# Where the sample states are read: one pass behind the projection, or two halves inside it

## What is computed

```python
S_new = jnp.exp(b_last)[..., None] * S + jnp.einsum('bshk,bshv->bhkv', k_dec, vc)
o_inter = jnp.einsum('bthk,bhkv->bthv', qc * jnp.exp(b), S)
```

## Time and profile before

| | |
|---|---|
| median of 3 runs | 1629.11 us (1628.82 to 1630.61) |
| profiled execution | 1628.45 us |
| its span | 1626.7 us |
| TensorE busy | 1551.4 us, 95% |
| VectorE, ScalarE, GpSimd busy | 1280.9, 976.4, 148.4 us |
| mean DMA rate | 274 GB/s |
| mixer of layer 0, projection and output | about 17 to 170 us |
| mixer of layer 1 | about 392 to 545 us |
| experts | from about 586 us on |

### The profile page before, as it was taken

One profiled execution on the slowest core, in us unless ns is written; L12 is line 12 of the kernel. 1 busy time (PEld: TensorE's weight loads), 2 busy tenths in 40 slices (PEclk: granted clock), 3 DMA queues, 4 the chain that ended last, 5 costly groups with the idle time before them and its releaser, 6 DMA issues.

```text
span 1626.7 us, 23700 instructions
## 1 busy us (share of the span) xinstructions
PE 1551.4 (95%) x8504; PEld 1330.3 (82%) x8504; DVE 1280.9 (79%) x1192; ACT 976.4 (60%) x832; POOL 148.4 (9%) x115
## 2 busy tenths in 40 slices
PE   7989899998999969999999999999999999999996
PEld 6989899998989858778788788787787787887884
DVE  6874666656575368989989989989989888888885
ACT  6463433334454256776776776676776676677672
POOL 2000560000000000200200200200200200200100
PEclk9997999999997879999999999999999999999999
DMA  9451676454433159999999999999999999999990
GB/s 305 141 169 37 215 229 203 155 179 132 155 107 109 53 204 339 366 359 344 366 361 336 359 364 340 364 368 338 355 370 346 349 366 341 349 366 351 344 388 29
DMA packets 216397, 445.21 MB, mean 274 GB/s; under 512 B 7568, under 2 KB 63304, under 8 KB 216352
## 3 DMA queue, kind: packets, MB, share of 16 engines
q1 hardware_dynamic: 208480, 421.72, 72.9%
q0 software_dynamic: 4960, 16.47, 3.2%
q10 hardware_dynamic: 2912, 6.42, 1.3%
HBM read 437.58 MB, written 7.06 MB: 273 GB/s over the span
## 4 chain that ended last, share of the span: by engine, by line
PE 73%; DVE 11%; issue 9%; ACT 4%; DMA 2%; ACTq 0%; DVEq 0%; POOLq 0%; SPq 0%
PE ps L1474 22%; PE ps L1476 21%; PE ps L1475 21%; DVE w_lo L873 7%; ACT w_hi L532 2%; PE ps L1646 2%; DMA raw<-in_moe_w_dram 1%; PE ps L1550 1%; PE ps L1839 1%; PE ps L1499 1%; DVE ex_g L1386 1%; DVE xT L1375 1%; ACT ex_silu L807 1%; PE ps L1799 0%; PE ps L1751 0%
## 5 line engine op out<-in xcount | busy, mean ns | idle before, releaser
L873 DVE TENSOR_TENSOR w_lo<-raw,w_hi 128x2048 fp32r<-128x2048 f32 x401 | 941.5, 2364 | 174.5 <-ACT w_hi L532 172.2
L532 ACT ACTIVATE w_hi<-raw 128x2048 fp32r<-128x2048 f32 x401 | 762.6, 1917 | 257.2 <-PE ps L1476 210.8
L1474 PE MATMUL ps<-w_hi,xg 128*128 128x512 f32 x896 | 360.6, 402 | 11.3 <-DVE w_lo L873 10.0
L1475 PE MATMUL ps<-w_lo,xg 128*128 128x512 f32 x896 | 352.4, 393 | 0.0
L1476 PE MATMUL ps<-w_hi,xg 128*128 128x512 f32 x896 | 352.3, 393 | 0.0
L1474 PE MATMUL ps<-h_hi,w_hi 128*128 128x264 f32 x736 | 216.1, 294 | 18.4 <-DVE h_lo L921 8.4
L1474 PEld LDWEIGHTS ps<-w_hi,xg 128*128 128x128 f32 x896 | 169.1, 189 | 55.9 <-DVE w_lo L873 22.2
L1476 PE MATMUL ps<-h_hi,w_lo 128*128 128x264 f32 x736 | 211.0, 287 | 0.0
L1475 PE MATMUL ps<-h_lo,w_hi 128*128 128x264 f32 x736 | 211.0, 287 | 0.0
L1476 PEld LDWEIGHTS ps<-w_hi,xg 128*128 128x128 f32 x896 | 168.8, 188 | 37.8
L1475 PEld LDWEIGHTS ps<-w_lo,xg 128*128 128x128 f32 x896 | 169.4, 189 | 33.0
(11 more groups left out here) (299 smaller groups left out, 1604.9 us busy)
## 6 DMA issues: line engine op xcount, KB each, us to landing
raw<-in_moe_w_dram SPq DMA_DIRECT2D x336, 1024.0 KB, 6.0
raw<-in_ffn_w_dram SPq DMA_DIRECT2D x33, 1024.0 KB, 5.4
raw<-in_w_in_dram SPq DMA_DIRECT2D x24, 1024.0 KB, 5.9
raw<-in_w_out_dram SPq DMA_DIRECT2D x8, 1024.0 KB, 5.0
vb<-v_rows_scratch POOLq DMA_DIRECT2D x16, 256.0 KB, 5.1
out_dram<-hstate POOLq DMA_DIRECT2D x2, 2048.0 KB, 12.7
hstate<-in_state_hgrn_dram POOLq DMA_DIRECT2D x1, 2048.0 KB, 11.3
x_rows<-in_x_prompt_dram SPq DMA_DIRECT2D x1, 1024.0 KB
```

Of the source, the lines that this page charges most:

```text
L532: act.activation(w_hi[:, s, :], raw[:, r, :], ACT.Copy).then_inc(hi_made, 1)
L873: dve.tensor_tensor(w_lo[:, s, :], raw[:, r, :], w_hi[:, s, :].bitcast(F32), ALU.subtract).then_inc(split, 1)
L1474: pe.matmul(out, l_hi, r_hi, start=start, stop=False)
L1475: pe.matmul(out, l_hi, r_lo, start=False, stop=False)
```

## The change

Level k still stands behind unit 6 + k up to level 5. The reads become two halves of four samples. The first stands behind level 4 of unit 10, the second behind level 5 of unit 11, and each has a turn among banks 0 to 3; ScalarE evicts the results to a small tile (`states_out`). A half is 1 MB and lies in `half_state`, where the token-major values and keys will stand later, so GpSimd can load it early: the first half ahead of the mixer (in layer 1 after the final state of layer 0 is done), the second when the first is read. ScalarE's load is gone. The reload for the new states of layer 1 is issued by GpSimd behind the first gather of the experts. Levels 6 and 7 stand ahead of the transposes of the values; VectorE's low parts of units 13 and 14 move behind a gate product and behind the prompt's gate products; the gate product with the root (L1153) moves ahead of the last widening; the sums of squares stand ahead of the final state. Two waits fall away: TensorE's for the samples' outputs ahead of the merges and ScalarE's for the reads ahead of the next norm. The diff, with its context cut:

```diff
--- before.py
+++ after.py
@@ -60,7 +60,7 @@
-GATES_BEHIND = {7: (0, 1), 8: (2, 3, 4), 9: (5, 6, 7)}
+GATES_BEHIND = {7: (0, 1), 8: (2, 3, 4), 9: (5, 6, 7), 10: ("states",), 11: ("states too",)}
 TILE_TURN, GATE_TURN = [], {}
@@ -68,6 +68,7 @@
 TURNS = len(TILE_TURN) + len(GATE_TURN)
+STATE_TURN = [GATE_TURN["states"], TURNS - 1]
@@ -144,6 +145,7 @@
         vrow = at("vrow", end("xc"), [HEADS * P])
+        half_state = at("half_state", end("sc"), [NSAMPLE // 2 * HEADS, P])
         s_fin = at("s_fin", end("xc"), [HEADS, P])
@@ -203,6 +205,7 @@
         tmp = small[:, 48:160]
+        o_s = tmp[:, 0:32].rearrange("p (h b) -> p h b", h=HEADS)
         key_s = small[:, 168:200].rearrange("p (h b) -> p h b", h=HEADS)
@@ -420,6 +423,14 @@
             def mixer(l):
+                if l:
+                    pool.wait_ge(fin_done, l)
+                for half in range(2):
+                    if half:
+                        pool.wait_ge(st_read, NSAMPLE * l + NSAMPLE // 2)
+                    pool.dma_start(half_state[:, :, :],
+                                   state_hgrn[l, 4 * half:4 * half + 4].rearrange(
+                                       "b h k v -> k (b h) v")).then_inc(st_landed, 16)
                 pool.wait_ge(vrow_ready, l + 1)
@@ -488,8 +499,10 @@
             pool.wait_ge(y_done, 2 * DC + DC * FF_STEPS)
-            pool.wait_ge(st_read, NSAMPLE * DEPTH)
+            pool.dma_start(hstate[:, :, :], state_hgrn[1].rearrange("b h k v -> k (b h) v")
+                           ).then_inc(st_again, 16)
             values_begin(1)
+            pool.wait_ge(st_again, 32)
             pool.wait_ge(blocks_ready, 1)
@@ -579,8 +592,6 @@
             def norm_hi(n):
-                if n == 1:
-                    act.wait_ge(st_read, NSAMPLE)
                 for c in range(DC):
@@ -615,6 +626,18 @@
+                def states_out(half):
+                    bank = ps[:, STATE_TURN[half] % 4, :]
+                    act.wait_ge(z_done, TURNS * l + STATE_TURN[half] + 1)
+                    ins = act.activation(o_s[:, :, 4 * half:4 * half + 4],
+                                         bank[:, 0:16].rearrange("p (h b) -> p h b", h=HEADS),
+                                         ACT.Copy)
+                    if half == 0:
+                        ins.then_inc(act_step, 1)
+                        steps[0] += 1
+                        ins = act.activation(tmp[:, 64:96], bank[:, 32:64], ACT.Copy)
+                    ins.then_inc(z_free, 1)
+
                 if l:
@@ -624,7 +647,12 @@
                     for n in GATES_BEHIND.get(u - SPLIT, ()):
-                        gate(n)
+                        if n == "states":
+                            states_out(0)
+                        elif n == "states too":
+                            states_out(1)
+                        else:
+                            gate(n)
                     if l == 0 and u == SPLIT - 1:
@@ -668,12 +696,6 @@
                         act.activation(zx[:, :, :], zx[:, :, :], ACT.Sqrt).then_inc(om_root, 1)
-                    if u == IN_UNITS + SPLIT - 1:
-
-                        act.wait_ge(used, ib + IN_UNITS)
-                        act.dma_start(hstate[:, :, :],
-                                      state_hgrn[l].rearrange("b h k v -> k (b h) v")
-                                      ).then_inc(st_landed, 16)
                 act.wait_ge(v_turned, l + 1)
@@ -1098,7 +1120,7 @@
                 for u in range(IN_UNITS + SPLIT):
-                    if u >= EARLY[l]:
+                    if EARLY[l] <= u <= IN_UNITS:
                         lo(ib + u)
@@ -1145,12 +1167,13 @@
                                                ALU.mult))
-
+                        lo(ib + u)
+
+                dve.wait_ge(om_root, l + 1)
+                link(dve.tensor_tensor(lev[0][:, :, :], lev[0][:, :, :], zx[:, :, :], ALU.mult))
                 widen(7, queries_too=False)
-                dve.wait_ge(om_root, l + 1)
-                link(dve.tensor_tensor(lev[0][:, :, :], lev[0][:, :, :], zx[:, :, :], ALU.mult))
                 for j in range(HEADS):
@@ -1177,11 +1200,9 @@
                 link(dve.tensor_tensor(zg[:, :, :], zg[:, :, :], cum[:, :, :], ALU.mult))
-                dve.wait_ge(st_read, NSAMPLE * (l + 1))
-                link(dve.tensor_tensor(own, ps[:, 5, 0:HEADS * NSAMPLE].rearrange(
-                    "p (j b) -> p j b", j=4), zv[:, :, NPROMPT:T], ALU.mult))
-                dve.tensor_tensor(heads[:, :, NPROMPT:T], ps[:, 5, 32:64].rearrange(
-                    "p (j b) -> p j b", j=4), own, ALU.add).then_inc(o_ready, 1)
+                dve.wait_ge(z_free, 4 + TURNS * (l + 1))
+                link(dve.tensor_tensor(own, own, zv[:, :, NPROMPT:T], ALU.mult))
+                dve.tensor_tensor(heads[:, :, NPROMPT:T], o_s, own, ALU.add).then_inc(o_ready, 1)
                 for n in range(HEADS):
@@ -1192,6 +1213,7 @@
                                       zg[:, h, 0:NPROMPT], ALU.mult).then_inc(hz_ready, 1)
+                lo(ob + 2)
                 for h in range(HEADS + 1):
@@ -1564,6 +1586,24 @@
+                def read_states(half):
+                    turn = STATE_TURN[half]
+                    pe.wait_ge(st_landed, 16 * (2 * l + half + 1))
+                    pe.wait_ge(z_free, TURNS * l + turn + 1)
+                    if half == 0:
+                        pe.matmul(ps[:, turn % 4, 32:64], ones[:, :], tmp[:, 32:64], start=True,
+                                  stop=True)
+                    for b in range(4):
+                        for h in range(HEADS):
+                            col = NPROMPT + 4 * half + b
+                            out = 4 * h + b
+                            ins = pe.matmul(ps[:, turn % 4, out:out + 1],
+                                            half_state[:, HEADS * b + h, :],
+                                            zq[:, h, col:col + 1], start=True, stop=True)
+                        ins.then_inc(st_read, 1)
+                    pe.wait_ge(st_read, NSAMPLE * l + 4 * (half + 1))
+                    pe.sem_inc(z_done, 1)
+
                 def level(k):
@@ -1605,7 +1645,9 @@
                         level(u - 6)
-                    for n8 in GATES_BEHIND.get(u, ()):
+                    if u == 10:
+                        read_states(0)
+                    for n8 in GATES_BEHIND.get(u, ()) if u < 10 else ():
                         j = n8 % 4
@@ -1613,6 +1655,9 @@
+                read_states(1)
+                level(6)
+                level(7)
                 pe.wait_ge(z_free, 4 + TURNS * (l + 1))
@@ -1622,12 +1667,6 @@
                 ins.then_inc(v_turned, 1)
-                level(6)
-                level(7)
-
-                pe.wait_ge(sc_taken, PRODUCTS * l + 14)
-                pe.matmul(ps[:, 5, 0:HEADS * NSAMPLE], ones[:, :], tmp[:, 32:64], start=True,
-                          stop=True)
                 pe.wait_ge(kd_ready, l + 1)
@@ -1638,14 +1677,6 @@
                 pe.wait_ge(vrow_ready, l + 1)
-                pe.wait_ge(st_landed, 16 * (l + 1))
-                for b in range(NSAMPLE):
-                    for h in range(HEADS):
-                        col = NPROMPT + b
-                        out = 32 + NSAMPLE * h + b
-                        ins = pe.matmul(ps[:, 5, out:out + 1], hstate[:, HEADS * b + h, :],
-                                        zq[:, h, col:col + 1], start=True, stop=True)
-                    ins.then_inc(st_read, 1)
                 pe.wait_ge(sc_taken, PRODUCTS * (l + 1))
@@ -1654,23 +1685,23 @@
                               stop=True).then_inc(o_done, 1)
+                for h in range(HEADS):
+                    pe.wait_ge(o_sq, HEADS * l + h + 1)
+                    pe.wait_ge(hz_ready, HEADS * l + h + 1)
+                    pe.matmul(ps[:, h, 0:T], ones[:, :], zf[:, h, :], start=True, stop=True
+                              ).then_inc(o_ssq, 1)
+
                 pe.wait_ge(kd_tok_ready, l + 1)
                 ins.then_inc(fin_done, 1)
-                for h in range(HEADS):
-                    pe.wait_ge(o_sq, HEADS * l + h + 1)
-                    pe.wait_ge(hz_ready, HEADS * l + h + 1)
-                    pe.matmul(ps[:, h, 0:T], ones[:, :], zf[:, h, :], start=True, stop=True
-                              ).then_inc(o_ssq, 1)
                     pe.wait_ge(m_split, DC * l + n + 1)
-                pe.wait_ge(o_ready, l + 1)
                 for c in (1, 2, 3, 0):
```

## The result

The changed kernel takes **1633.22 us** (median of 10 runs, 1630.01 to 1635.9); the kernel before, on the same chip, 1628.96 us (10 runs, 1622.08 to 1630.98). The ratio is 1.003, 95% interval 1.0016 to 1.0044: slower by 0.3%, a small difference, but the interval leaves out 1. The profiled execution took 1632.13 us, its span is 1630.4 us.

The account below looks back on a forecast made before the run. TensorE, busy 95% of the span, bounds the kernel, with one-column reads at half clock in the mixers. Per layer, -5.0 us at full clock plus 7.0 of low clock gave +2.0, +4.0 in all: 1633 us, range 1629 to 1642.

Parts of the forecast that it names:

- its clock: Low-clock price added to the full-clock terms: 2.7 us for each half of the reads, 1.6 at the merges, per layer.
- (a): First half of the reads, behind level 4 in unit 10: end of level 5 comes 4.4 us later at full clock.
- (b): Second half of the reads, between unit 11 and level 6: 6.1 us against 6.0 before, at full clock.
- (c): End of level 6 to first merge product: VectorE sets it, 17.5 us instead of 27.0, gain 9.5 at full clock.
- my upper end of 4.9: Highest clock price per half: reads wholly low, 3.3 us, plus a low stretch behind them, 1.6 us.
- (d): DMA loads: second half lands in 5.5 to 7 us, in time; at worst 2.7 us a layer; reload hidden.
- Full clock: Rival: dense units on both sides keep the clock full inside the projection; -10 us, 1619; chance 0.20.
- The clock rule: The skill's gate rule, taken by TensorE's busy share: full clock through the reads, the sum without clock price.
- Short dips: Rival: one short dip per half, none at the merges; -1.8 us a layer, 1625.5; chance 0.22.
- Late half: Rival: the second half of the states lands late; +2.7 us a layer on top of the forecast, 1638; chance 0.05.
- ScalarE: Rival: its table loads and copies set gate and outputs before the merges; gain 7, not 9.5 us a layer, 1638; chance 0.04.

Follow-up runs that it names:

- e1: Changed kernel with each one-column read widened to 128 columns by a broadcast query; 1615.77 us, ratio to the kernel before 0.9941.
- e3: Changed kernel with the final state put back ahead of the sums of squares; 1628.81 us, ratio to the kernel before 1.0006.
- e4: Kernel before with its reads over 128 broadcast columns, at their old place behind the transposes; 1612.18 us, ratio 0.9911.
- e5: Changed kernel with reads over 128 broadcast columns and the final state ahead of the sums of squares; 1616.11 us, ratio 0.992.
- e7: Kernel before with levels 6 and 7 ahead of the values' transposes and reads over 128 broadcast columns behind them; 1612.59 us, ratio 0.99.
- e6: Kernel before with only levels 6 and 7 moved ahead of the values' transposes, reads narrow and behind; 1628.6 us, ratio 0.9996.
- e8: Changed kernel with its reads over 32 broadcast columns; 1632.87 us, ratio to the kernel before 1.0031.
- e2: Changed kernel without 30 of the 32 reads of each layer, so the samples' outputs are incomplete; 1611.49 us, ratio 0.9908.
- e10: Changed kernel with reads over 128 broadcast columns, the second half's four samples all between levels 6 and 7; 1620.81 us, ratio 0.9955.
- e9: Changed kernel with reads over 128 broadcast columns, the second half split: two samples ahead of level 6, two behind it; 1618.29 us, ratio 0.9939.

## Why the prediction came out

The forecast was 1633.0, the run gave 1633.2, in the range and with the likeliest sign. By its steps, in layer 0 (start of level 4 unchanged):

| step | predicted, with its clock | measured |
|---|---|---|
| (a) end of level 5 | +4.4 + 2.7 = +7.1 | +7.2 (112.55 to 119.77) |
| (b) end of level 5 to end of level 6 | +0.1 + 2.7 = +2.8 | +3.8 (6.0 to 9.8) |
| (c) end of level 6 to first merge | -9.5 + 1.6 = -7.9 | -7.2 (27.0 to 19.8) |
| sum | +2.0 | +3.8 |

- **(a)** held, and so did its clock: reads 1.1 us over 3.6, unit 11 8.0 us instead of 6.1, together 3.0 against 2.7.
- **(b)** held at full clock. Its clock was under-sized: reads 2.4 us over, level 6 1.7 over, 4.1 us against 2.7, near my upper end of 4.9. This is the term that was mis-sized most. My price was for reads that run low in part, or a dip of some 3 us behind them; the low stretch lasted 14 us and took in most of the reads, level 6, a wait of 1.39 us, level 7 and most of the transposes. Under level 7 and the transposes it is hidden behind VectorE but for the 0.62 us of (c).
- **(c)** held: VectorE's chain from the end of level 6 was 15.4 us, forecast 14.9; the 0.5 more is the wait of 0.62 us for ScalarE's copy (L719), which I had left out. ScalarE's work up to that copy starts at the end of the values' transposes, and those ended late because they ran low: in layer 1 of e1, where they ran at full clock (1.04 us, not 1.74, for the first eight passes), VectorE does not wait there at all. The dip of (c) is 3.49 + 2.20 - 3.9 = 1.8 us, forecast 1.6.
- **(d)** held. Landing of the halves, the tile's view, after:

```profile
L431 POOL DMA_DIRECT2D half_state<-in_state_hgrn_dram x4: 1151/1158/1222, 12.1 to 488.4; - x4
...
DMA to landing us min/median/max: 6.8/9.0/15.7
```

The load that had to hurry, the second half, landed in 7.3 us in layer 0 and 6.8 in layer 1; estimated were 5.5 to 7. (I read the earlier trace rows as loads only: ScalarE's two took 11.1 and 11.7 us, the 13.9 is another transfer of that tile.) The median is 9.0 because the first halves, which had time, took 10.7 and 15.7 us beside busy DMA engines (share 1.08 and 0.96, against 0.50 and 0.47 for the second halves). The second half was asked for at 109.5 and needed at 119.6, and no wait of TensorE was put down to it. The low clock itself gave it 2 us of that room; in e1 it had 8.2 us, landed in 7.0 and was there too. The reload ahead of the experts did not delay the first gather (4.0 us).
- **The sum.** The +3.8 of layer 0 had become +7.3 us at the norm behind layer 1's mixer, where +4.0 was forecast. That the total was +3.7 in the profiled executions is due to the router's 3.3 us, which I had not forecast. So the mechanism held, but the forecast was 1.8 us a layer short (1.0 in (b), 0.7 in (c), 0.1 in (a)), and that the total came out within 0.2 us is luck. Whether the router did the same in the other nine runs behind the median, no trace shows.

**Rivals.** Full clock (1619, 0.20): out as a forecast, since narrow reads lower it even between dense units. But e1 makes the condition true inside the projection, and its price of -10 us held: -9.6 us by the ratio, -11.8 by the medians beside each other. The clock rule read by the profile's busy share is out with it (e1). Short dips: out in this execution, where the one in the projection lasted 6.5 us and the one behind it 14; e3's trace, with the second half at full clock, comes nearer to it. Late half: out. ScalarE: 0.62 us of it is real, and it comes from the low clock of the transposes.

What the change was worth apart from the clock under the reads: e1 against e4, e5 against e7. With wide reads, the new order is some 3.5 us dearer than the old one (0.9941 against 0.9911; 0.992 against 0.99; the intervals overlap a little in both pairs). From level 4 to the norm behind the mixer the traces agree: 62.7 us in each layer of e5, 61.2 and 61.3 in e7, so 2.8 us. The size is rough and the sign likely. The two also differ in the loads and in the order of VectorE's low parts and one gate product, so that it is the place of the reads alone is argued (the first half, paid in full, against 5 us free), not shown. The levels as they fell in e6 are worth nothing.

## What to carry to other kernels

A TensorE group can be busy for 1.00 and still be what slows everything behind it: compare the count of passes in a stretch, and its granted clock, before you move the group. Here the change that moved the one-column reads cost 4 us, and widening them by a broadcast, with no other work changed, gained 15 to 17 us in either order; the best kernels of this study are the old order with wide reads, 1612.2 and 1612.6 us. And filler work belongs where TensorE would wait for another engine's chain, not ahead of that chain's start.

## What the runs showed of the hardware beyond that

- The granted clock fell with no idle time but a drain's 0.30 us before it: from 1.00 to 0.50 at 107 us, 2.5 us into one-column passes that show busy 1.00 (after). Reads over 32 columns (e8) did the same, over 128 (e1) not. And the same idle time does not give the same clock: 2.17 us left it full in layer 0 of e3 and low in e5; 1.21 us ahead of level 6 (e2) cost 1.7 us in layer 0 and 0.4 in layer 1.
- At full clock a pass costs nearly the same for 1, 32 and 128 columns: the 32 passes of a half took 3.69 us (e3, second half), 3.71 (e8, second half) and 3.79 (e1, second half), 0.115 to 0.118 us a pass.
- The router's stretch from its first products to the gathered tokens' transposes came out in two sizes in the profiled executions, with no edit in it: 22.3 to 22.8 us (after, e1, e3, e4, e7, e8, e10) and 24.5 to 26.0 (before, e2, e5, e6, e9), the first with most of its small products at full clock, the second at half. So a single trace can move by 3 us there, about what this change is worth.
- Loads of 1 MB from GpSimd's queue landed in 6.8 and 7.3 us at a DMA share of about 0.5, and in 10.7 and 15.7 us at a share of about 1 (after); ScalarE's two loads of 2 MB took 11.1 and 11.7 us (before). So the same 1 MB took from 6.8 to 15.7 us, the longer times where other transfers filled the engines.
